# Sixteen of the 31 taps of one convolution channel group, multiplied on ScalarE and summed on GpSimd

## What is computed

```python
def _dwconv(u, w):            # depthwise, width 31, padding 15 on both sides
    return lax.conv_general_dilated(u, w[:, None, :], window_strides=(1,), padding=[(15, 15)], ...)

def _even_mix(h, w_in, a_conv_w, a_conv_b, a_ln_g, a_ln_b, a_pw_w, a_pw_b, b_fw, w_out):
    a_val, a_glu, a_gate, b_val, b_gate = _split(h @ w_in, [512, 512, 512, 512, 512])
    u = a_val * jax.nn.sigmoid(a_glu)
    u = jax.nn.silu(_layernorm(_dwconv(u, a_conv_w) + a_conv_b, a_ln_g, a_ln_b))
    y_a = (u @ a_pw_w + a_pw_b) * jax.nn.silu(a_gate)
    y_b = _fourier_mix(b_val, b_fw) * jax.nn.silu(b_gate)
    return jnp.concatenate([y_a, y_b], axis=-1) @ w_out
```

## Time and profile before

| | |
|---|---|
| median of 3 executions | 2182.71 us (2178.2 to 2186.56) |
| profiled execution | 2182.54 us, its span 2180.7 us |
| PE busy | 2072.9 us (95%) |
| DVE busy | 1321.8 us (61%), of it 180.3 us in 120 taps of L1587 |
| ACT busy | 753.8 us (35%) |
| POOL busy | 195.2 us (9%) |
| stage `ein`, from PE's first unit to the start of `four` | about 1068 to 1379.5 us of the span |

### The profile page before, as it was taken

The page is one execution under the profiler, slowest core; times in us unless marked ns, Lnnn a source line. Parts: engine busy times, 40 slices in busy tenths (PEclk is TensorE's granted clock), DMA queues, the critical chain, the costliest instruction groups (busy, mean ns, idle before and its releaser), DMA issues. The chain is left out here.

```text
span 2180.7 us, 25839 instructions
## 1 busy us (share of the span) xinstructions
PE 2072.9 (95%) x10208; PEld 1696.8 (78%) x10208; DVE 1321.8 (61%) x2243; ACT 753.8 (35%) x1419; POOL 195.2 (9%) x170
## 2 busy tenths in 40 slices
PE   6999999999999999999889999789998999999796
PEld 4877887888888888888578888578876777888685
DVE  7378867632742652563778888675354346777634
ACT  4265644311311310322531212452133235555432
POOL 2033211000000000000110000000011012232101
PEclk9999999999999999999899999899999999999898
DMA  3112012312321321321201232025121121101312
GB/s 140 52 30 88 30 38 79 135 49 78 106 78 49 136 78 50 106 108 49 112 30 39 76 87 75 11 70 196 39 100 68 58 64 37 37 25 39 111 45 81
DMA packets 42871, 156.92 MB, mean 72 GB/s; under 512 B 4352, under 2 KB 9088, under 8 KB 41472
## 3 DMA queue, kind: packets, MB, share of 16 engines
q1 hardware_dynamic: 40304, 146.49, 19.7%
q10 hardware_dynamic: 2448, 8.79, 1.0%
HBM read 135.34 MB, written 19.92 MB: 71 GB/s over the span
## 5 line engine op out<-in xcount | busy, mean ns | idle before, releaser
L173 PE MATMUL banks<-u2H,wH 128*128 128x512 f32 x736 | 297.2, 404 | 12.6 <-DVE u2L L427 4.9
L174 PE MATMUL banks<-u2L,wH 128*128 128x512 f32 x736 | 289.2, 393 | 0.0
L175 PE MATMUL banks<-u2H,wL 128*128 128x512 f32 x736 | 288.6, 392 | 0.0
L173 PE MATMUL banks<-aH,wH 128*128 128x512 f32 x640 | 251.0, 392 | 0.1
L175 PE MATMUL banks<-aH,wL 128*128 128x512 f32 x640 | 249.2, 389 | 0.0
L174 PE MATMUL banks<-aL,wH 128*128 128x512 f32 x640 | 249.2, 389 | 0.0
L168 DVE TENSOR_TENSOR wL<-raw,wH 128x1024 fp32r<-128x1024 f32 x153 | 186.7, 1221 | 89.9 <-ACT wH L163 89.8
L163 ACT CAST wH<-raw 128x1024 fp32r<-128x1024 f32 x153 | 159.7, 1045 | 230.7 <-DMA raw<-in_wstream 225.8
L173 PE MATMUL banks<-mH,wH 128*128 128x512 f32 x512 | 200.3, 391 | 0.6 <-DVE mL L429 0.6
L174 PE MATMUL banks<-mL,wH 128*128 128x512 f32 x512 | 200.0, 391 | 0.0
L175 PE MATMUL banks<-mH,wL 128*128 128x512 f32 x512 | 199.9, 390 | 0.0
(11 more groups left out here) (297 smaller groups left out, 4011.0 us busy)
## 6 DMA issues: line engine op xcount, KB each, us to landing
raw<-in_wstream SPq DMA_DIRECT2D x153, 512.0 KB, 3.6
mod_w<-in_mod_w SPq DMA_DIRECT2D x48, 512.0 KB, 5.4
x_scratch<-h SPq DMA_DIRECT2D x2, 4096.0 KB, 11.3
gt<-gates_scratch SPq DMA_DIRECT2D x8, 640.0 KB, 4.4
h<-in_x SPq DMA_DIRECT2D x4, 1024.0 KB, 10.6
hm<-in_x SPq DMA_DIRECT2D x1, 4096.0 KB, 13.7
h<-x_scratch SPq DMA_DIRECT2D x1, 4096.0 KB, 12.2
xo<-x_scratch SPq DMA_DIRECT2D x1, 4096.0 KB, 12.3
```

The lines of the kernel that those rows point to most:

```text
L173: first = pe.matmul(out, aH, bH, start=start, stop=False)
L174: pe.matmul(out, aH, bL, start=False, stop=False)
L175: return first, pe.matmul(out, aL, bH, start=False, stop=stop)
```

## The change

For the last channel group (chunk 3) taps 15 to 30 leave DVE. ACT multiplies the shifted input by each of these weights (`scale_tap`), two after each of the gate units 8 to 15, into `side_sum` (the first) or one of two buffers `side_tap`. POOL adds the 15 others to `side_sum`, one after the other. DVE adds `side_sum` to the group's `conv_out` once, in v = 17. Two pairs of semaphores are merged to make room for the new ones. The side buffers lie in the last parts of `bH` and `bL`, which are written later.

```diff
+        SIDE = 16
+        SIDE_TAPS = range(TAPS - SIDE, TAPS)
+        side_sum = sb("side_sum", [CONV_OUT], A_B + 40 * KB - 5184)
+        side_tap = [sb("side_tap0", [CONV_OUT], A_B + 20 * KB - 5184), sb("side_tap1", [CONV_OUT], A_B + 40 * KB - 2 * 5184)]
+        side_scaled, side_added = sem("side_scaled"), sem("side_added")
...
+            def scale_tap(n):
+                c, tap = HALF - 1, SIDE_TAPS[n]
+                dst = side_tap[(n - 1) % 2][:] if n else side_sum[:]
+                if n > 2:
+                    act.wait_ge(side_added, n - 2)
+                act.activation(dst, conv_in[:, c, tap:tap + CONV_OUT], ACT.Copy, scale=pcol("conv_w", c * TAPS + tap))\
+                    .then_inc(side_scaled, 1)
+
             for i in range(0, 4):
                 for s, buf in enumerate((sig, val)):
                     gate(i, s, buf)
                     split_hi(act, E0 + 10 + 2 * i + s)
+                    for n in range(2):
+                        scale_tap(2 * (2 * i + s) + n)
...
+            for n in range(1, SIDE):
+                pool.wait_ge(side_scaled, n + 1)
+                if n > 1:
+                    pool.wait_ge(side_added, n - 1)
+                pool.tensor_tensor(side_sum[:], side_sum[:], side_tap[(n - 1) % 2][:], ALU.add).then_inc(side_added, 1)
...
+            TAPS_OF = [TAPS] * (HALF - 1) + [TAPS - SIDE]
...
-                    open_ = [c for c in range(chunks) if steps[c] < TAPS]
+                    open_ = [c for c in range(chunks) if steps[c] < TAPS_OF[c]]
...
                     taps(4 if v < 18 else HALF * TAPS, HALF)
+                    if v == 17:
+                        dve.wait_ge(side_added, SIDE - 1)
+                        dve.wait_ge(conv_step, latest[HALF - 1] + 1)
+                        dve.tensor_tensor(conv_out[:, HALF - 1, :], conv_out[:, HALF - 1, :], side_sum[:], ALU.add)\
+                            .then_inc(conv_step, 1)
                     fold_low(v - 16)
...
-            pe.wait_ge(conv_step, HALF * TAPS)
+            pe.wait_ge(conv_step, HALF * TAPS - SIDE + 1)
```

More of the change, by code:

```diff
@@ L1453, in build @@
         bL = sb("bL", [HALF, TOK], A_B + 20 * KB, F32R)
-        (ctx_loaded, x_spilled, mod_ready, mod_step, ein_done, ein_drained, ci_ready, conv_step,
-         folded, fold_step, b_hi, b_lo) = (sem(v) for v in (
-             "ctx_loaded x_spilled mod_ready mod_step ein_done ein_drained ci_ready conv_step folded "
+        SIDE = 16
[3 more added lines that the diff above has]
+        side_scaled, side_added = sem("side_scaled"), sem("side_added")
+        (ctx_loaded, x_spilled, mod_step, ein_done, ein_drained, ci_ready, conv_step,
+         fold_step, b_hi, b_lo) = (sem(v) for v in (
+             "ctx_loaded x_spilled mod_step ein_done ein_drained ci_ready conv_step "
              "fold_step b_hi b_lo").split())
@@ L1519, in ein_act @@
                 split_hi(act, E0 + 18 + v)
-                act.wait_ge(folded, v + 1)
+                act.wait_ge(fold_step, 3 * v + 3)
                 act.copy(bH[:, v, 0:SEQ], bf[:]).then_inc(b_hi, 1)
@@ L1541, in ein_dve @@
                                                  par[:, PC[name]:PC[name] + 8], ALU.add, ALU.mult)
-                    m.then_inc(mod_ready, 1)
-            dve.wait_ge(mod_ready, 4)
+                    m.then_inc(mod_step, 1)
+            dve.wait_ge(mod_step, 2 + 4)
             norm3.wait(dve, "ready", 2 * KC)
@@ L1557, in fold @@
                 dve.tensor_tensor(bf[:, 0:512], bt[:, 0:512], bt[:, 512:1024], ALU.subtract).then_inc(fold_step, 1)
-                dve.wait_ge(fold_step, 2 * g + 1)
+                dve.wait_ge(fold_step, 3 * g + 1)
                 dve.tensor_tensor(bt[:, 0:512], bt[:, 0:512], bt[:, 512:1024], ALU.add).then_inc(fold_step, 1)
-                dve.wait_ge(fold_step, 2 * g + 2)
+                dve.wait_ge(fold_step, 3 * g + 2)
                 dve.tensor_tensor(bf[:, 512:768], bt[:, 0:256], bt[:, 256:512], ALU.subtract)
-                dve.tensor_tensor(bf[:, 768:1024], bt[:, 0:256], bt[:, 256:512], ALU.add).then_inc(folded, 1)
+                dve.tensor_tensor(bf[:, 768:1024], bt[:, 0:256], bt[:, 256:512], ALU.add).then_inc(fold_step, 1)
             def fold_low(g):
```

## The result

The changed kernel takes 2189.61 us against 2182.69 us (medians of 16 executions each): +6.9 us, a ratio of 1.003 with a 95% interval of 1.0023 to 1.0037. It is slower, by less than half a per cent. The profiled execution has a span of 2189.0 us.

The account below looks back on a forecast made before the run. PE, busy 95% of the span, was taken as the bound, with DVE becoming it after the change. PE's delay of 16.3 us less 9.2 us saved gave +7.0 us, so 2189.5 us; range 2180 to 2197 us.

Parts of the forecast that it names:

- The gain: Wait of PE at the start of `four`: removing v = 18's eleven taps saves 9.2 us, leaving about 5.8 us.
- ACT free of charge: ACT behind the gate units: two products, 2.6 us, hide in its 3.69 us wait for PE's next tile; nothing added.
- The price of an addition: DVE's splits and taps in v = 8 to 15: each 1295-element POOL addition takes 2.81 us of DVE time.
- L: DVE time taken by one POOL addition of 1295 elements: 2.81 us, bounds 2.71 and 3.03.
- The base of 1.07: DVE time taken by each 512-element POOL instruction, read at the end of the program: 1.07 us.
- Free time and lead: DVE from v = 8: 16.15 us of waits absorb part, `fold(0)` comes 26.3 us later; weights of unit 18 have 10.0 us slack.
- the work per iteration: DVE in v = 8 to 15: a split and 7 taps take 11.58 us, eight iterations 92.6 us.
- The clock: PE's granted clock after long waits for weights: a unit's slow start is absorbed while PE waits for DVE anyway.
- rival B: Clock falls at a long wait ahead of unit 17 or 18 and its loss stays: +9.7 us, 2192.2 us; chance 25%.
- the likeliest case: Additions make DVE the bound, PE's slow starts are absorbed: 2189.5 us, bounds 2188 to 2193; chance 50%.
- the total of 7.0: Whole kernel: PE starts unit 18 later by 16.3 us, 9.2 us are saved: +7.0 us.
- The mechanism: DVE instructions with two SBUF inputs, taps and splits, stand still when they meet a POOL addition; 2.81 us each.

Follow-up runs that it names:

- spread_and_sums_first: Kernel before the change, no offload: v = 18's eleven taps placed earlier, PE's sums moved ahead of its wait for the last fold_low; 2165.52 us, ratio 0.9927.

## Why the prediction was right, point by point

- **The gain.** 9.23 us for the eleven taps of v = 18. Shown: the wait at the sums went from 15.0 to 5.8 us in the changed kernel, and the change without additions gains 9.6 us.
- **ACT free of charge.** Shown by the same run. Its products took 1.36 to 1.38 us (1.3 predicted), and its wait ahead of a next tile was 1.1 us, as worked out.
- **The price of an addition.** L = 2.81 predicted, 2.72 to 2.74 measured. The base of 1.07 was 1.03, and POOL's first addition of 1295 elements took 2.98 us, not 3.03. The exclusive lock of the Trainium skill ("SBUF — State Buffer", section "Who interferes with whom"), taken for the whole POOL instruction as the prediction took it, would be 2.98; the trace gives 0.25 less, at 512 elements (1.29 and 1.03) as at 1295. The price in the sum was 15 x 0.08 = 1.2 us too high.
- **Free time and lead.** DVE reached `fold(0)` 24.5 us later in its own measure (133.3 us from v = 8 instead of 108.8), 26.3 predicted. Of these 1.8 us too many, 1.2 are the price above. The rest is nearly all a slip in the work per iteration: the 10.44 us of seven taps run 0.09 us past the start of the next instruction, so eight iterations without a pause are 0.7 us shorter than 8 x 11.58. The lateness of PE at the end of unit 19 was 16.0, 16.3 predicted.
- **The clock.** I took it that a slow start is absorbed by the next wait, with rival B for a long wait ahead of unit 17 or 18. It fell ahead of unit 17: B's condition held, and the likeliest case was wrong in this. B's price was too high, because PE worked at half clock for 3.1 us there and not for 5.4. DVE's split for unit 18 ended at 1348.78 + 1.22 = 1350.0, but PE ended unit 17, begun at half clock after 6.0 us of standing, only at 1365.33 - 13.78 = 1351.55: 1.5 us of the 16.0 are the clock's.
- **Luck in the number.** DVE's lateness was put 1.8 us too high and the clock's part 1.5 too low. The two cancel, so the total of 7.0 is closer than its terms. The waits also lay otherwise than forecast: three, the longest of 6.0 us, 10.6 in all instead of 16 in pieces of 3.4, because additions bunched (none in one iteration, four in the next) and the clock took the rest.
- **The total in this stage.** From the split of v = 8 to the first sum: 1384.8 - 1213.40 = 171.4 us, before 1379.5 - 1214.88 = 164.6, +6.8 us. The two profiled spans differ by 8.3. The changed kernel's was 1.5 us ahead at v = 8 and loses 3.0 from the first sum to the end, in code that is the same in both. There its granted clock was 0.77 from 1660 to 1675, where before, 5.3 us earlier, the same stretch had 1.00; 61 matmuls were done in it before and 47 after. Whether the change brings this about is not shown.

```profile
1654.70:1669.70 15.00, 12.33 (x61) 10.29 (x61) 2.36 (x2) 2.26 (x3) 0.00 (x0) 1.00 0.11 35
1660.00:1675.00 15.00, 12.34 (x47) 9.94 (x46) 2.36 (x2) 2.26 (x3) 0.00 (x0) 0.77 0.11 35
```

- **The mechanism.** That an addition stops DVE by its reading is shown by the memsets (no cost), the shorter additions (cost by length) and the copies (cost with one input). Whether the split and the taps are stopped because they have two SBUF inputs was not tried in this stage; it rests on the earlier trace rows.

## What to carry to other kernels

Before work moves from DVE to POOL, look whether DVE's instructions have two SBUF inputs and POOL's read SBUF: then POOL's time can be DVE's time too, here all but 0.25 us of each addition, and one addition on POOL (2.73 us of DVE) cost more than the tap that it saved (1.49). Look first for free time on the same engine: the eleven taps that stood in the way fitted into pauses that the profile showed, and that was worth more than the offload. And ask of each wait whether it must stand ahead of everything behind it: moving one wait of PE gave 7.5 us by itself and 5.4 us on top of the spread taps, where it also kept the clock up.

## What the runs showed of the hardware

- 45 memsets of 1295 elements on POOL, 1.18 us each, left DVE's taps at 1562 ns, and 15 copies of the same length took 1.0 us each from DVE, where the copy alone takes 1.27.
- With work waiting on both engines, 14 of the changed kernel's 15 additions got in after the DVE instruction that was running, one of them even ahead of a split (4.00 us instead of 1.22). The other stood through five taps and a split and took 11.02 us; so no order is certain, and the additions bunched into some iterations.
- PE's clock was at 0.76 within the slice that began 1.6 us after PE fell idle at 1282.4, and at 0.50 for the next 6 us of work; after the 1.7 us that PE stood ahead of unit 13 it stayed at 1.00. In spread_and_sums_first, where PE stood 0.5 us at the start of `four`, it stayed at 1.00 there; all the other executions worked for 3.6 to 5.4 us at 0.50 behind that wait, which cost them 1.8 to 2.7 us.
